# Two feed-forward products out of three joined into one 512-column product, with the halves added afterwards

## The reference, cut to what matters

```
def swiglu(x, wg, wu, wd):
    return (jax.nn.silu(x @ wg) * (x @ wu)) @ wd
...
x = layer_norm(DN_ALPHA * x + 0.5 * swiglu(x, ffn1_wg[i], ffn1_wu[i], ffn1_wd[i]), ln_g[i, 0], ln_b[i, 0])
```

## Time and profile before

| what | value |
|---|---|
| median of 3 runs | 2130.39 us (2130.28 to 2131.53) |
| span of the profiled execution, first to last instruction | 2131.0 us |
| TensorE busy | 2102.4 us, 99% |
| VectorE busy | 1492.2 us, 70% |
| ScalarE busy | 1111.1 us, 52% |
| mean granted clock of TensorE | 0.996 of full |

### The profile page before, as it was taken

One profiled execution on the slowest core, in us unless ns is written; L12 is line 12 of the kernel. 1 busy time (PEld: TensorE's weight loads), 2 busy tenths in 40 slices (PEclk: granted clock), 3 DMA queues, 4 the chain that ended last, 5 costly groups with the idle time before them and its releaser, 6 DMA issues.

```text
span 2131.0 us, 36321 instructions
## 1 busy us (share of the span) xinstructions
PE 2102.4 (99%) x15424; PEld 1905.9 (89%) x15424; DVE 1492.2 (70%) x2246; ACT 1111.1 (52%) x1749; POOL 8.6 (0%) x14
## 2 busy tenths in 40 slices
PE   9999999999999999999999999999999999999998
PEld 8999899999999999899998887988888899888997
DVE  5777867777677676467777558665555678778776
ACT  5445664446444654464447658353333467666454
POOL 0000000000000000000000000000000000000000
PEclk9999999999999999999999999999999999999999
DMA  8665445664566422156653211234443444214541
GB/s 330 244 255 208 164 180 220 239 256 169 225 255 241 171 102 87 60 209 231 254 226 119 99 61 41 78 141 158 157 155 149 175 174 152 106 41 178 195 182 60
DMA packets 51282, 359.28 MB, mean 169 GB/s; under 512 B 5680, under 2 KB 5808, under 8 KB 8496
## 3 DMA queue, kind: packets, MB, share of 16 engines
q1 hardware_dynamic: 49680, 351.30, 43.8%
q10 hardware_dynamic: 1440, 5.65, 0.7%
HBM read 355.88 MB, written 1.05 MB: 167 GB/s over the span
## 4 chain that ended last, share of the span: by engine, by line
PE 89%; DVE 5%; ACT 4%; issue 1%; DMA 0%; SPq 0%; ACTq 0%; DVEq 0%
PE ps L1030 9%; PE ps L1029 9%; PE ps L1028 9%; PE ps L3007 5%; PE ps L3009 5%; PE ps L3008 5%; PE ps L1112 4%; PE ps L1113 4%; PE ps L1114 4%; PE ps L461 2%; PE ps L462 2%; PE ps L463 2%; PE ps L1329 2%; PE ps L1344 2%; PE ps L2670 2%; PE ps L2672 2%
## 5 line engine op out<-in xcount | busy, mean ns | idle before, releaser
L400 DVE TENSOR_TENSOR wl<-ring,wh 128x1024 fp32r<-128x1024 f32 x380 | 452.8, 1220 | 161.8 <-ACT wh L394 161.6
L1028 PE MATMUL ps<-xs,wh 128*128 128x256 f32 x1664 | 471.1, 283 | 1.2 <-DVE wl L434 0.9
L1030 PE MATMUL ps<-xs,wh 128*128 128x256 f32 x1664 | 470.9, 283 | 0.0
L1029 PE MATMUL ps<-xs,wl 128*128 128x256 f32 x1664 | 470.9, 283 | 0.0
L394 ACT ACTIVATE wh<-ring 128x1024 fp32r<-128x1024 f32 x380 | 379.5, 1050 | 96.4 <-PE ps L1114 72.8
L1028 PEld LDWEIGHTS ps<-xs,wh 128*128 128x128 f32 x1664 | 319.0, 192 | 5.9 <-DVE wl L434 1.8
L1029 PEld LDWEIGHTS ps<-xs,wl 128*128 128x128 f32 x1664 | 319.0, 192 | 4.1 <-issue 0.2
L1030 PEld LDWEIGHTS ps<-xs,wh 128*128 128x128 f32 x1664 | 319.0, 192 | 0.0
L1112 PE MATMUL ps<-wh,hh 128*128 128x512 f32 x440 | 173.0, 393 | 0.8 <-DVE hl L1227 0.8
L1113 PE MATMUL ps<-wl,hh 128*128 128x512 f32 x440 | 172.4, 392 | 0.0
L1114 PE MATMUL ps<-wh,hl 128*128 128x512 f32 x440 | 171.2, 389 | 0.0
(11 more groups left out here) (577 smaller groups left out, 4488.0 us busy)
## 6 DMA issues: line engine op xcount, KB each, us to landing
ring<-wstream SPq DMA_DIRECT2D x331, 1024.0 KB, 4.9
cond_ctx<-crow ACTq DMA_DIRECT2D x3, 512.0 KB, 10.3
CN<-consts ACTq DMA_DIRECT2D x1, 1056.0 KB, 9.1
X<-xin SPq DMA_DIRECT2D x4, 256.0 KB, 5.6
ring<-wstream SPq DMA_DIRECT2D x4, 256.0 KB, 6.5
ring<-wstream SPq DMA_DIRECT2D x2, 512.0 KB, 8.8
X<-cin ACTq DMA_DIRECT2D x1, 1024.0 KB, 8.6
out<-X SPq DMA_DIRECT2D x4, 256.0 KB, 2.9
```

The lines of the kernel that those rows point to most:

```text
L400: dve.tensor_tensor(lo, w, hi.bitcast(F32), ALU.subtract).then_inc(low_part, tiles_done)
L1028: pe.matmul(out, wh[:, w, c, :], x_hi, start=start, stop=False, skip_group_check=True)
L1029: pe.matmul(out, wl[:, w, c, :], x_hi, start=False, stop=False, skip_group_check=True)
L1030: return pe.matmul(out, wh[:, w, c, :], x_lo, start=False, stop=True, skip_group_check=True)
```

## The change

It changes tiles t = 2 to 21 of the five feed-forwards on 256 tokens. The high and the low part of x lie side by side in memory (`x[:, c, 0:2, :]`), so high weights times high x and high weights times low x become one product of 512 columns into a whole bank, and low weights times high x is added to its first 256 columns. Gate and up have a bank each, and two pairs of banks (4 and 5, 6 and 7) take turns. The second half of each bank must then be added to the first: ScalarE copies both second halves (128x512) to `gu_sum` in SBUF, and VectorE adds the two first halves. Silu, the convolution and the product read `gu_sum` in place of PSUM. `gu_sum` lies where `rstd` and `lnv` lie, which are used at other times. Some semaphores are joined (the constants and `p`; zeros and eps), and the conditioning sums are called one at a time; their place in VectorE's order stays.

```diff
+        gu_sum = put("gu_sum", [2, 2, T], over=("norm_rows", 0))
...
+        def halves_bank(t):
+            return 4 + 2 * ((t + 1) % 2)
...
+            def gate_up_in_halves(t):
+                for k in range(2):
+                    w, out = BUF[i0 + 3 * t + k], ps[:, halves_bank(t) + k, :]
+                    pe.wait_ge(low_part, i0 + 3 * t + k + 1)
+                    for c in range(KC):
+                        pe.matmul(out, wh[:, w, c, :], x[:, c, :, :].rearrange("p a n -> p (a n)"), start=(c == 0), stop=False,
+                                  skip_group_check=True)
+                        mm = pe.matmul(out[:, 0:T], wl[:, w, c, :], x[:, c, 0, :], start=False, stop=True, skip_group_check=True)
+                mm.then_inc(gate_up_done, 1)
...
             for t in range(2, NT):
-                gate_up(t)
+                gate_up_in_halves(t)
                 down(t - 1)
...
(ScalarE, hidden)
-                n, k, gate = NT * f + t, t % 4, ps[:, 4 + t % 4, 0:T]
+                n, k, gate = NT * f + t, t % 4, gu_sum[:, t % 2, 0, :] if t >= 2 else ps[:, 4 + t, 0:T]
                 act.wait_ge(gate_up_done, n + 1)
+                if t >= 2:
+                    b = halves_bank(t)
+                    act.activation(gu_sum[:, t % 2, :, :], ps[:, b:b + 2, T:2 * T], ACT.Copy).then_inc(half_copied, 1)
+                    act.wait_ge(halves_added, halves(f, t))
...
(VectorE, hidden)
+            def add_halves(t):
+                b = halves_bank(t)
+                dve.wait_ge(half_copied, halves(f, t))
+                dve.tensor_tensor(gu_sum[:, t % 2, :, :], ps[:, b:b + 2, 0:T], gu_sum[:, t % 2, :, :], ALU.add
+                                  ).then_inc(halves_added, 1)
...
-                gate, up = ps[:, 4 + k, 0:T], ps[:, 4 + k, T:2 * T]
+                gate, up = (gu_sum[:, t % 2, j, :] if t >= 2 else ps[:, 4 + t, j * T:(j + 1) * T] for j in range(2))
+                if t >= 2:
+                    add_halves(t)
```

More of the change, by code:

```diff
@@ L286, in build_program @@
         MOD = put("MOD", [2, 48, 2])
-        rstd = put("rstd", [2 * T])
-        lnv = put("lnv", [2 * T])
+        norm_rows = put("norm_rows", [4 * T])
+        rstd = put("rstd", [2 * T], over=("norm_rows", 0))
+        lnv = put("lnv", [2 * T], over=("norm_rows", 8 * T))
+        gu_sum = put("gu_sum", [2, 2, T], over=("norm_rows", 0))
         hsc = put("hsc", [3, 4, T])
@@ L314, in build_program @@
         in_ident = sem("in_ident")
-        in_params, in_x0, in_consts, in_p, in_ctx, in_wab, out_done = (
-            sem(n) for n in ("in_params", "in_x_first", "in_consts", "in_p", "in_ctx", "in_wab", "out_done"))
+        in_params, in_x0, in_tables, in_ctx, in_wab, out_done = (
+            sem(n) for n in ("in_params", "in_x_first", "in_constants_and_p", "in_ctx", "in_wab", "out_done"))
         in_x = [in_x0] + [sem(f"in_x_pair{q}") for q in (1, 2, 3)]
@@ L324, in build_program @@
         x_even = sem("x_high_even_block")
-        zeros_set = sem("zeros_set")
+        constants_set = sem("zeros_then_eps_set")
         in_piece = [sem(f"in_slot0_piece{q}") for q in range(3)] + [sem("in_slot1_first_half")]
@@ L332, in build_program @@
         mean_done, centred, squared, var_done = (sem(n) for n in ("mean_done", "centred", "squared", "var_done"))
-        ln_done, rstd_done, z_normed, eps_set = (sem(n) for n in ("ln_done", "rstd_done", "z_normed", "eps_set"))
+        ln_done, rstd_done, z_normed = (sem(n) for n in ("ln_done", "rstd_done", "z_normed"))
         z_paired_pool = sem("z_paired_by_pool")
@@ L523, in dve_ada, with dve_ada_one @@
                                             accum_out=MOD[:, layer, block, j:j + 1])
-        def dve_ada_both(f, n):
+        def dve_ada_one(f, n, j):
             a = len(ADA_PAIRS) * f + n // 2
-            if n == 0:
+            if n == 0 and j == 0:
                 if f == 0:
@@ L531, in dve_ada_both @@
                 dve.wait_ge(cond_ready[1], (1, 2, 2, 3)[f])
-            if n % 2 == 0:
+            if n % 2 == 0 and j == 0:
                 dve.wait_ge(*loaded(ADA_AT[a]))
             layer, block = divmod(2 * a + n % 2, 48)
-            for j in range(2):
-                done = dve_ada(a, n % 2, layer, block, j)
-            if n % 2:
+            done = dve_ada(a, n % 2, layer, block, j)
+            if n % 2 and j:
                 done.then_inc(ada_done, 1)
@@ L1019, in dve_ln_columns, with halves @@
             done.then_inc(ln_cols_made, 1)
+        def halves_bank(t):
+            return 4 + 2 * ((t + 1) % 2)
+        def halves(f, t):
+            return (NT - 2) * min(f, 4) + t - 1
         def pe_ffn(f, name, normed=None):
@@ L1040, in warm_up @@
             def warm_up():
-                pe.wait_ge(zeros_set, 1)
+                pe.wait_ge(constants_set, 1)
                 for n in range(4):
@@ L1188, in act_ffn @@
                 if f == 0 and t == 1:
-                    act.dma_start(CN[:, P:], consts[:, P:]).then_inc(in_consts, 16)
-                    act.dma_start(PT_[:, :, :, :], pin).then_inc(in_p, 16)
+                    act.dma_start(CN[:, P:], consts[:, P:]).then_inc(in_tables, 16)
+                    act.dma_start(PT_[:, :, :, :], pin).then_inc(in_tables, 16)
                 if f == 0 and t == 2:
@@ L1252, in dve_ffn @@
                 if f < 4 and (t + 1) // 2 in ADA_PAIRS:
-                    dve_ada_both(f, t + 1 - 2 * ADA_PAIRS.start)
+                    for j in range(2):
+                        dve_ada_one(f, t + 1 - 2 * ADA_PAIRS.start, j)
                 if beside and t == 1:
@@ L3775, in pe_program @@
                 if i == 0:
-                    pe.wait_ge(in_consts, 16)
-                    pe.wait_ge(in_p, 16)
+                    pe.wait_ge(in_tables, 32)
                 pe_token_norm(f"ffn1_{i}", lambda: pe_ple_proj(i, "a"))
@@ L3792, in act_program @@
             act_ffn(0, "ffn1_0", X[:, 0], after=tiles("ab_in"), late=third("ab_in"))
-            act.wait_ge(eps_set, 1)
+            act.wait_ge(constants_set, 2)
             act_token_norm("ffn1_0")
@@ L3822, in dve_program @@
         def dve_program():
-            dve.memset(Z[:, 0, 0:2, :], 0.0).then_inc(zeros_set, 1)
+            dve.memset(Z[:, 0, 0:2, :], 0.0).then_inc(constants_set, 1)
             dve.memset(ln_eps[:, 0:1], 1e-5)
             dve.memset(ln_eps[:, 2:3], 1e-5 / ALPHA ** 2)
-            dve.memset(ln_eps[:, 1:2], 1e-6).then_inc(eps_set, 1)
+            dve.memset(ln_eps[:, 1:2], 1e-6).then_inc(constants_set, 1)
             half = lambda c: 0.5
             dve_ffn(0, "ffn1_0", X[:, 0], half, after=tiles("ab_in"), late=third("ab_in"))
-            dve.wait_ge(in_consts, 16)
+            dve.wait_ge(in_tables, 32)
             dve_token_norm("ffn1_0")
```

1 line of the change is left out of this document (added).

## The result

The changed kernel takes 2154.2 us (median of 4 runs, 2153.30 to 2156.01) against 2130.93 before (4 runs, 2130.28 to 2131.53). The ratio is 1.0109, 95% interval 1.0097 to 1.0121: slower by 1.1%. The profiled executions span 2152.2 us against 2131.0, both at a mean granted clock of 0.996.

What follows compares the result with a forecast made beforehand. TensorE was taken as the bound (8.50 us an iteration), with the VectorE and ScalarE loop close behind (7.56) and passing it after the change. 2131.0 + 7.7 (f = 0 to 3) + 13.8 (l1) = 2152.5, forecast 2152 us; range 2137 to 2168.

Steps and rivals of the forecast that it cites:

- The loops: VectorE and ScalarE's loop per iteration: 8.75 us in f = 0 to 3, 9.24 in l1, against TensorE's 8.32.
- rival (1): Each loop holds 0.2 us more than the sum of its pieces, giving about 2168 us; chance 0.11.
- Rival (2): The loop of f = 0 to 3 is at or under 8.32 us, so only l1 loses: 2136; chance 0.08.
- Rival (3): VectorE's 1.47 us of idle per iteration takes up the add and silu wait, TensorE stays the bound: 2120; chance 0.06.
- Rival (5): The time changes by no more than 0.2%, about 4 us, costs lying between rivals (2) and (3); chance 0.05.
- the pair of products: In gate_up, one product of 512 and one of 256 columns take 0.348 us in place of 0.360, 18 us in all.
- the nearest row: Trace row of groups of 512, 256, 256, 512 columns, 0.697 us each, half of it taken as 0.348 a pair.
- the later end: In f = 0 to 3, the path from gate_up(21) to `hh` grows by 1.4 us through copy, add and handoffs.
- the waits: TensorE waits 4.1 us in each of f = 0 to 3, from near t = 10 until t = 20.
- +13.8: In l1, the side tap of t = 21 comes at 2129.9 in place of 2116.17.
- waits for `wl` at gate_up: Sign of the forecast: TensorE's iterations 8.32 us until about t = 10, then 8.75, waiting for `wl`.
- rival 4: TensorE's many short waits bring its clock to the lower level in late iterations, giving 2185 us; chance 0.03.

Runs made afterwards that it cites:

- x2: The changed kernel with the conditioning sums of f = 0 to 3 over 64 of their 1024 columns; 2142.29 us, 1.0042 of the kernel before.
- x5: The changed kernel with each iteration's two conditioning sums made one iteration later, behind the add and behind the product; 2143.23 us, 1.0055 of the kernel before.
- x3: The changed kernel with l1 in the old form, only f = 0 to 3 having the new products, copy and add; 2139.99 us, 1.0039 of the kernel before.
- x4: The changed kernel with VectorE's gate row product in l1 moved from ahead of the add to behind it; 2138.31 us, 1.0030 of the kernel before.
- x9: The changed kernel with only TensorE's product order altered, to 512, 512, 256, 256; 2152.24 us, 1.0089 of the kernel before.
- x6: The changed kernel with the moves of x4 and x5 together; 2127.66 us, 0.9980 of the kernel before.
- x8: x7 with TensorE's products in the order 512, 512, 256, 256; 2114.18 us, 0.9919 of the kernel before.
- x1: The changed kernel without copy and add, second halves left out of the sum; 2120.66 us, 0.9943 of the kernel before.
- x7: x6 with copy and add each made in two halves of 128x256, gate first; 2124.02 us, 0.9966 of the kernel before.
- x10: x7 with eight products of 512 first, then eight of 256; 2115.88 us, 0.9921 of the kernel before.

## Why the prediction was right

**The mechanism** (VectorE waits for silu behind the add, the next low parts stand behind that wait, TensorE waits for them) is shown: by x2 and x5 for f = 0 to 3, by x3 and x4 for l1, and by x9 for both, since a quicker TensorE gains next to nothing.

**The loops.** f = 0 to 3: 8.75 predicted, 8.74 measured; l1: 9.24 and 9.25. The add at 0.69 (686 ns), silu at 0.42 (418) and handoffs of 0.04 held, so rival (1), handoffs, has no place. Rival (2), only l1 suffers, would have wanted a loop of at most 8.32 in f = 0 to 3. Rival (3), the add in VectorE's idle, is what x6 to x8 make true by moving other work, not what the change does by itself. Rival (5), no change by 0.2%, is out at 1.1%.

**The mis-sized term** is the pair of products: 0.348 predicted, 0.353 measured. The step that failed was to take as "the nearest row" for any mixture; there two products of 256 stand together, in the change each stands alone. The gain with TensorE as the bound is 12 us (x1), not 18. By the Trainium skill (TensorE: Matmul & The Clock Gate, Back-to-back issue gap) 2.5 ns go with a product. The trace differs: the gate_up of x1 shows (5.75 - 5.64)/16 = 7 ns, that of x8 (5.75 - 5.56)/16 = 12 ns.

That f = 0 to 3 still came out nearly as predicted is no luck: where a loop through VectorE is the bound, the end of a stage does not depend on TensorE. From the first product of gate_up(2) to the first `tok_st` each of these stages takes 170.9 us before, 168.6 in x1, 170.0 in x2 and x5, and 173.0 in the changed kernel. So the gain is 2.3, the later end costs 1.4 and the waits cost 3.0, where the prediction had 3.6, 1.4 and 4.1: a gain that is smaller by 1.3 brings waits that are smaller by 1.1. The waits began at t = 12, not near 10, because the slower TensorE used up VectorE's lead more slowly. The four lose 8.5 (7.7 predicted).

That the whole sum came out within 0.1% is in part luck. The five stages lost 2.3 us more than predicted, and what lies outside them, which the prediction put at nothing, came out 2.6 shorter, for the most part because the clock was lower at other places in the two executions.

**l1** was predicted at +13.8. The side tap of t = 21 came 14.0 later by l1's own doing; another 1.3 arose behind it (below), 15.3 in all. Where TensorE would wait was wrong: "waits for `wl` at gate_up" is true of f = 0 to 3, but in l1, without the last wait of 2.9, 9.5 of 13.2 us are waits for `hl` ahead of down. `hl` stands in the same loop, so the time is the same.

**The clock** (rival 4) stayed up in the late iterations. Windows of the changed kernel in ffn1_0 and l1 (length, busy us of PE, PEld, DVE, ACT, POOL, then the granted clock):

```profile
90.00:178.00 88.00, 87.48 (x448) 72.11 (x447) 73.08 (x103) 42.89 (x61) 0.00 (x0) 1.00 0.64 242
1990.00:2120.00 130.00, 121.71 (x620) 99.08 (x619) 99.23 (x128) 66.72 (x98) 0.00 (x0) 1.00 0.42 157
```

With waits of 0.2 to 0.65 us in every iteration it is 1.00. The Trainium skill (TensorE: Matmul & The Clock Gate, A second HAM failure mode: psum-queue depth-cycling) tells of another kernel in which frequent micro-idles between groups of matmuls made the clock swing. These windows do not show it.

## What to carry to other kernels

An engine with 30% of idle time can be full all the same: add up the loop that comes back to the same instruction, waits for the other engine included, and compare that with the bound engine's iteration. When work is put on such an engine, ask what stands behind the new wait, and move independent work into it: the place of one or two instructions was worth 16 and 11 us here, where the products themselves gain 12. And when a product's price is read from a mixture, read it from the same order.

## What the runs showed of the hardware

At the end of l1 in the changed kernel TensorE idles 2.88 us before the last down and then runs at the lower level:

```profile
2139.00 0.64 PE L1132 MATMUL ps<-wh,hh 128*128 128x512 f32 x1 [2.88 <-DVE hl L1259]
2139.43 0.63 PE L1133 MATMUL ps<-wl,hh 128*128 128x512 f32 x1
...
2142.42 0.46 PE L1134 MATMUL ps<-wh,hl 128*128 128x512 f32 x1
2142.72 0.39 PE L1132 MATMUL ps<-wh,hh 128*128 128x512 f32 x1
```

The products start 0.43 us apart until 2142.42, then 0.23; the granted clock of 2140 to 2142 is 0.50, that is 1.2 of 2.4 GHz. From the end of that wait to the first product of the layer norm it is 5.60 us (2139.00 to 2144.60); in x4, where the same wait lasted 2.61 us and the clock stayed at 1.00, it is 4.28 (2125.20 to 2129.48), so some 1.3 us of l1's 15.3 are this. The window of x4:

```profile
2124.00:2126.00 2.00, 0.80 (x4) 0.70 (x5) 0.57 (x2) 1.70 (x2) 0.00 (x0) 1.00 0.00 0
```

So a cost of the lower clock came in where nobody had looked for it, behind a long wait and not in the many short ones. But the length of that wait does not settle it. In x2, x5 and x6 the clock fell to 0.50 about the end of a wait of 2.87, 2.84 and 2.76 us at this place. In x9 the wait is 2.86, the clock stayed at 1.00, and from the end of the wait to the layer norm it takes 4.28 as in x4:

```profile
2139.43 0.47 PE L1134 MATMUL ps<-wh,hh 128*128 128x512 f32 x1 [2.86 <-DVE hl L1261]
```

```profile
2140.00:2142.00 2.00, 2.00 (x10) 1.65 (x9) 1.56 (x4) 0.13 (x1) 0.00 (x0) 1.00 0.00 0
```

What decides between the two stays open.

The second surprise is the price of order: the same 512- and 256-column products take 0.353 a pair when they alternate and 0.348 or 0.349 in twos or eights, worth 10 us between x7 and x8 and 8 between x7 and x10.
